# Two of the seven products of a paired feed-forward pass take both halves of their moving data in one 512-column matmul

## The chip, the core and the metric

The kernel runs on one core of a Trainium2 chip, as one program for two transformer stacks. The metric is the device time of one execution in microseconds (us). Before the change it is 3205.59 us, the median of three runs (3205.07 to 3207.72). The engines of the core work in parallel and meet through semaphores: TensorE (PE, with its weight loads as PEld), VectorE (DVE), ScalarE (ACT), GpSimd (POOL), and SyncE (SP), which issues most DMAs.

## The reference, cut to what matters

All tensors are float32, 512 tokens of width 1024. Among attention and mixer layers there are six gated feed-forward layers of hidden width 2816, and the change touches the input side of these:

```python
gate, up = jnp.split(h @ w_ffn_in[l], 2, axis=-1)          # two layers of the first stack
f = (jax.nn.silu(gate) * up) @ w_ffn_out[l]

def _swiglu(h, wg, wu, wd):                                # four of the second stack
    return (jax.nn.silu(h @ wg) * (h @ wu)) @ wd
```

## The kernel before

A float32 product is made of three products of a reduced format (fp32r). Each operand is split into a high part, which ScalarE casts, and a low part, which VectorE or GpSimd gets by subtracting the high part. A product then is w_hi x high + w_hi x low + w_lo x high, accumulated in a PSUM bank of 128 x 512 float32.

The input side of a feed-forward layer (a pass, below) has 22 gate tiles and 22 up tiles of 128 columns. The first five of each are done plainly, as ten units. The other 17 of each are "pairs" p = 0 to 16: a gate tile and the up tile of the same hidden columns are computed together as a 2 x 2 block product by a Strassen-like scheme with seven products instead of eight. The weight of a pair is split in A11, A12 (gate row) and A22 and A21 (up row), and four sums S1 to S4 are formed from them. The moving side has seven forms, B11, T1, T2, B21, B22, T3, T4, each of 4 k-tiles x 256 columns, made once a pass and kept with their high and low parts. The products in TensorE's order within `period(t, p)` are: A11 x B11, S1 x T1, A22 x T4 of the pair before (`fourth`), S2 x T2, A12 x B21, S4 x B22, S3 x T3. One product is twelve matmuls of 256 columns: `product` alternates high (L2771) and low (L2773) moving parts on the same w_hi block, four times, and then runs four with w_lo (L2777). Products on the chain go to bank 4 (odd p) or 6 (even p), `chain_bank`. The others share bank 5 or 7, `side_bank`: A12 x B21 in its left half, S1 x T1 and S4 x B22 in its right half.

While TensorE works on pair p, the other engines prepare pair q = p + 1 and finish p. Their order is the order of the code in each engine's `period`:

- ScalarE (L1161 on): a copy of the chain bank after product 1 (L1170, the first copy), S3's high part, A11's high part of q, a copy of S1 x T1 (`fifth_copy`, L1144), S1's high part, A22's, a copy of the chain (`sixth_copy`, L1153), S2's, A12's, then the silu of the gate (`silu_pair`, L1149), then S4's high part. High parts are L1127.
- VectorE (L1853 on): A11's low part, the sum S1, the hidden product of the pair before (L1835), A22's low part, the sum S2, the low parts of S1 of q and of S3 of p in one instruction of 1024 columns, A12's low part, the gate sum (L1895: side bank plus the two copies, which gives bank_free), the sum S4 (`fourth_sum`), the last half (L1850, which releases T4's product by st_u), the sum S3, the low parts of S2 and S4. Sums are L1806, low parts L1799.

The silu waits for bank_free of its pair. TensorE's w_lo matmuls of S3 in pair p wait for the low parts made in the same pair (`n_lo` 11 of a pair's seven counts, so four of the next seven); all the other weights are prepared a pair ahead. Each engine runs in order, so an instruction that waits holds all behind it. The first and last pairs are written out, and those between run as a hardware loop of two pairs (`pair_loop`). SyncE loads 512 KB for each row of a pair into a ring of four slots, released by st_sum and st_lo.

At the start of a pass VectorE builds the forms, ScalarE casts their high parts (`form_high`, L1124) and VectorE subtracts the low ones (`form_low`, L1795). A form's low part is written over its full value. High parts of B21 and B22 lie in the two halves of one four-tile region of mvh, those of T3 and T4 in the same region of mvl; these tiles are free once the ten plain units are done.

## Time and profile before

| | value |
|---|---|
| runs | 3205.07, 3205.59, 3207.72 us |
| the profiled execution | 3205.14 us, its span 3203.4 us |
| TensorE busy | 3157.5 us, 99% of the span, 19226 matmuls |
| TensorE's mean granted clock | 0.999 of full speed |
| VectorE, ScalarE, GpSimd busy | 2011.4, 1511.4, 1096.5 us |
| chain that ended last | TensorE 89%, VectorE 5%, ScalarE 2%, GpSimd 2%, issue 2% |
| matmuls of the paired part (L2771, L2773, L2777) | 8568 of 256 columns |

A matmul's row in the timeline has a modelled end: rows of consecutive matmuls overlap, so durations of matmuls are not their cost. The distance between starts is. VectorE's and ScalarE's rows also overlap by some hundredths of a microsecond, and there too the slot is the distance between starts.

### The profile page before, as it was taken

To read this page: it belongs to the slowest core of one execution; us is meant where nothing else is said; L and a number is where in the kernel's file an instruction comes from. 1 tells how busy PE (TensorE), PEld (TensorE's weight loads), DVE (VectorE), ACT (ScalarE), POOL (GpSimd) and SP (SyncE) were. 2 spreads that over 40 slices of the span, in tenths; PEclk is the share of its full clock that TensorE was granted. 3 is DMA by queue.
4 is the path that set the end of the run, shared out by engine and by line. 5 is a ranking of instruction groups with operands and counts; after the bars stand their busy time and mean duration, and the time that the engine had idled before them with its cause. 6 is when DMAs were issued, how large, how long until landed. Compare 5 with 4: busy or idle time off the path is not lost.

```text
span 3203.4 us, 53989 instructions
## 1 busy us (share of the span) xinstructions
PE 3157.5 (99%) x19226; PEld 2746.4 (86%) x19226; DVE 2011.4 (63%) x3103; ACT 1511.4 (47%) x2696; POOL 1096.5 (34%) x635
## 2 busy tenths in 40 slices
PE   9999999999999999999999999999999999999999
PEld 7678998786789987899888778998899887789987
DVE  4748874558488745888445247864688443348854
ACT  4655552557555524555333434552455333335542
POOL 5533014765340146500465341014400453350034
PEclk9999999999999999999999999999999999999999
DMA  4112332231123332232422122332232322122331
GB/s 158 53 47 87 109 114 97 86 103 53 47 86 105 112 104 80 80 105 92 154 92 86 53 73 80 105 118 98 79 103 90 129 94 71 61 86 93 103 118 66
DMA packets 82433, 294.27 MB, mean 92 GB/s; under 512 B 9035, under 2 KB 11467, under 8 KB 82028
## 3 DMA queue, kind: packets, MB, share of 16 engines
q1 hardware_dynamic: 80944, 286.06, 26.6%
q10 hardware_dynamic: 1340, 6.23, 0.5%
q8 instruction: 93, 1.52, 0.2%
q14 instruction: 56, 0.46, 0.1%
HBM read 290.15 MB, written 2.10 MB: 91 GB/s over the span
## 4 chain that ended last, share of the span: by engine, by line
PE 89%; DVE 5%; issue 2%; ACT 2%; POOL 2%; DMA 0%; SPq 0%; POOLq 0%; DVEq 0%; ACTq 0%
PE bank L2553 17%; PE bank L2555 17%; PE bank L2554 17%; PE bank L2777 10%; PE bank L2773 10%; PE bank L2771 10%; PE bank L3176 1%; PE bank L3156 1%; DVE w_lo L1799 1%; POOL w_lo L745 1%; ACT w_hi L1127 1%; PE bank L3263 1%; POOL diag L880 1%; PE bank L3018 1%; PE bank L3298 0%
## 5 line engine op out<-in xcount | busy, mean ns | idle before, releaser
L745 POOL TENSOR_TENSOR w_lo<-w_raw,w_hi 128x1024 fp32r<-128x1024 f32 (+1 forms) x334 | 790.3, 2375 | 1851.6 <-ACT w_hi L974 1807.6
L2553 PE MATMUL bank<-mvh,w_hi 128*128 128x512 f32 (+1 forms) x2774 | 1057.0, 381 | 10.3 <-DVE mvl L1708 2.9
L2555 PE MATMUL bank<-mvh,w_lo 128*128 128x512 f32 (+1 forms) x2774 | 1034.5, 373 | 0.0
L2554 PE MATMUL bank<-mvl,w_hi 128*128 128x512 f32 (+1 forms) x2774 | 1033.8, 373 | 0.0
L974 ACT ACTIVATE w_hi<-w_raw 128x1024 fp32r<-128x1024 f32 x333 | 351.1, 1058 | 799.2 <-PE bank L2555 759.3
L2553 PEld LDWEIGHTS bank<-mvh,w_hi 128*128 128x128 f32 x2774 | 522.3, 188 | 135.4 <-issue 35.2
L2555 PEld LDWEIGHTS bank<-mvh,w_lo 128*128 128x128 f32 x2774 | 522.2, 188 | 93.8
L2554 PEld LDWEIGHTS bank<-mvl,w_hi 128*128 128x128 f32 x2774 | 523.0, 189 | 84.9 <-issue 0.2
L1964 DVE TENSOR_TENSOR mvl<-big,mvh 128x512 fp32r<-128x512 f32 x108 | 255.8, 2368 | 327.4 <-ACT mvh L1261 327.4
L1127 ACT ACTIVATE w_hi<-w_lo_as 128x512 fp32r<-128x512 f32 x408 | 256.1, 630 | 202.1 <-DVE w_lo_as L1806 201.9
L2773 PE MATMUL bank<-y_as,w_hi 128*128 128x256 f32 x1224 | 306.9, 283 | 0.0
L2773 PE MATMUL bank<-big_as,w_hi 128*128 128x256 f32 x1224 | 306.8, 283 | 0.0
L1799 DVE TENSOR_TENSOR w_lo<-w_raw,w_hi 128x512 fp32r<-128x512 f32 x306 | 210.9, 689 | 95.1 <-ACT w_hi L1127 93.0
L1799 DVE TENSOR_TENSOR w_lo<-w_lo_as,w_hi 128x1024 fp32r<-128x1024 f32 (+1 forms) x216 | 250.6, 1162 | 11.2 <-DVE w_lo_as L1806 1.6
L2773 PEld LDWEIGHTS bank<-y_as,w_hi 128*128 128x128 f32 x1224 | 235.0, 192 | 0.2
L2773 PEld LDWEIGHTS bank<-big_as,w_hi 128*128 128x128 f32 x1224 | 234.9, 192 | 0.0
L2771 PE MATMUL bank<-mvl,w_hi 128*128 128x256 f32 x816 | 205.1, 284 | 1.7 <-DVE bank L1850 1.7
L2771 PE MATMUL bank<-mvh,w_hi 128*128 128x256 f32 x816 | 204.8, 283 | 0.0
L2771 PE MATMUL bank<-tab_as,w_hi 128*128 128x256 f32 x816 | 204.6, 283 | 0.0
L1127 ACT ACTIVATE w_hi<-w_raw 128x512 fp32r<-128x512 f32 x306 | 189.1, 618 | 3.5 <-issue 3.5
L880 POOL TENSOR_TENSOR diag<-diag,scr 128x512 f32<-128x512 f32 (+1 forms) x144 | 160.5, 1115 | 19.0 <-ACT scr L992 3.3
L2771 PEld LDWEIGHTS bank<-mvl,w_hi 128*128 128x128 f32 x816 | 156.5, 192 | 3.1 <-DVE bank L1850 2.9
(287 smaller groups left out, 4676.8 us busy)
## 6 DMA issues: line engine op xcount, KB each, us to landing
w_raw<-in_weights SPq DMA_DIRECT2D x537, 512.0 KB, 3.3
x<-in_x SPq DMA_DIRECT2D x8, 256.0 KB, 7.6
out_y<-y SPq DMA_DIRECT2D x8, 256.0 KB, 2.4
tab<-in_dist ACTq DMA_DIRECT2D x2, 640.0 KB
tab<-in_gmlp ACTq DMA_DIRECT2D x2, 640.0 KB
tab<-in_ret_dil ACTq DMA_DIRECT2D x1, 1280.0 KB
y<-in_p ACTq DMA_DIRECT2D x2, 512.0 KB, 3.5
y<-in_rotary ACTq DMA_DIRECT2D x1, 1024.0 KB
```

Of the source, the lines that this page charges most:

```text
L745: last = nc.gpsimd.tensor_tensor(w_lo[:, slot, at], w_raw[:, slot, at], w_hi[:, slot, at].bitcast(F32), ALU.subtract)
L880: nc.gpsimd.tensor_tensor(at, at, sq_at(name, i), ALU.add).then_inc(sq_used, 1)
L974: nc.scalar.activation(w_hi[:, slot, :], w_raw[:, slot, :], ACT.Copy).then_inc(w_hi_ready, 1)
L1127: nc.scalar.activation(st.hi(form), src, ACT.Copy).then_inc(st_hi, more)
L1799: nc.vector.tensor_tensor(st.lo(form, n), src, st.hi(form, n).bitcast(F32), ALU.subtract).then_inc(st_lo, more)
L1964: nc.vector.tensor_tensor(mvl[:, slot0 + s % 4, :], src, mvh[:, slot0 + s % 4, :].bitcast(F32), ALU.subtract).then_inc(mv_lo, 1)
L2553: nc.tensor.matmul(bank[:, at], hi, mvh[:, k, at], start=first, stop=False, skip_group_check=again)
L2554: nc.tensor.matmul(bank[:, at], hi, mvl[:, k, at], start=False, stop=False, skip_group_check=again)
L2555: return nc.tensor.matmul(bank[:, at], lo, mvh[:, k, at], start=False, stop=last, skip_group_check=again)
L2771: nc.tensor.matmul(bank, w, high[:, k, :], start=(begin and k == 0), stop=False, skip_group_check=True)
L2773: nc.tensor.matmul(bank, w, low[:, k, :], start=False, stop=False, skip_group_check=True)
L2777: last = nc.tensor.matmul(bank, w, high[:, k, :], start=False, stop=(k == 3), skip_group_check=True)
```

## The change

In pairs 1 to 15 (`wide`), the eight matmuls of a product with w_hi and the form B21 or B22 become four of 512 columns, whose moving operand holds the high part and the low part side by side (`both`). The bank then holds high-part columns at left and low-part columns at right. The two products take banks of their own: 0 and 1 in odd pairs, 2 and 3 in even pairs (`left_bank`, `side_bank`), with S1 x T1 in the left half of the second. VectorE adds the left halves of both banks to the copies (gate_begun), then the sum S4 is made, then it adds the right halves, which gives bank_free. To have high and low of B21 and of B22 adjacent, the low parts go beside the high parts, in mvh and mvl, and the high parts of T3 and T4 go where the full values and low parts of B21 and B22 were; ScalarE's casts of T3 and T4 therefore wait for form_lo. `down_first`, the start of the output side, waits for pair 15's bank_free, since it uses banks 0 to 3.

```diff
@@ -217,7 +217,8 @@
         gvar = small[:, 308:312]
         ret_vars = small[:, 232:248]
 
-        banks = [ctx.enter_context(nc.psum_tensor(f"bank{i}", [P, 512], F32)) for i in range(8)]
+        bank = ctx.enter_context(nc.psum_tensor("bank", [P, 8, 512], F32))
+        banks = [bank[:, i, :] for i in range(8)]
 
 
         x_loaded, p_loaded = [sem(f"x_loaded{i}") for i in range(KT)], sem("p_loaded")
@@ -287,6 +288,7 @@
         st_sum, st_hi, st_lo = sem("st_sum"), sem("st_hi"), sem("st_lo")
         st_prod, st_copy, st_u = sem("st_prod"), sem("st_copy"), sem("st_u")
         form_sum, form_hi, form_lo = sem("form_sum"), sem("form_hi"), sem("form_lo")
+        gate_begun = sem("gate_begun")
 
         def ge(eng, s, v):
 
@@ -589,7 +591,8 @@
                 m = 4 if name[0] == "a" else 0
                 wide = lambda t: t.rearrange("p a (b c) -> p (a b) c", c=S // 2)
                 late = [wide(t[:, m + j:m + j + 2, :]) for t in (mvh, mvl) for j in (0, 2)]
-
+                self.both = {f: t[:, m:m + 4, :].rearrange("p (j a) (b c) -> p j (a b) c", j=2, c=S // 2)
+                             for f, t in ((B21, mvh), (B22, mvl))}
 
                 def homes(y, big, scr):
                     ys = [wide(y[:, 2 * j:2 * j + 2, :]) for j in range(1, 4)]
@@ -602,7 +605,8 @@
                 pair = lambda t: t.rearrange("p (s a) (b c) -> p s (a b) c", s=2, c=S // 2)
                 self.normal = [pair(y[:, 2:6, :]), pair(big[:, FT:FT + 4, :])]
                 self.high = {B11: wide(scr_r[:, 8:10, :]), T1: tabs[0], T2: tabs[1]}
-                self.high.update(zip((B21, B22, T3, T4), late))
+                self.high.update({B21: late[0], B22: late[2], T3: self.low[B21], T4: self.low[B22]})
+                self.low.update({B21: late[1], B22: late[3]})
 
             def block(self, of, form, n=1):
                 at = (2 * (self.slot0 % RING) + form) % 8
@@ -626,7 +630,21 @@
                 return banks[4 if p % 2 else 6]
 
             def side_bank(self, p):
-                return banks[5 if p % 2 else 7]
+                return banks[7 if not self.wide(p) else 1 if p % 2 else 3]
+
+            def wide(self, p):
+
+                return 0 < p < PAIRS_ST - 1
+
+            def left_bank(self, p):
+                return banks[0 if p % 2 else 2]
+
+            def right(self, p):
+                return self.side_bank(p)[:, 0:S // 2] if self.wide(p) else self.side_bank(p)[:, S // 2:S]
+
+            def sides(self, p, part):
+                at = 0 if p % 2 else 2
+                return bank[:, at:at + 2, part * S // 2:(part + 1) * S // 2]
 
         def pair_loop(eng, first, last, body):
 
@@ -1121,6 +1139,8 @@
                 def form_high(form):
                     order = (B11, T1, T2, T3, B22, B21, T4)
                     act.wait_ge(form_sum, st.form0 + order.index(form) + 1)
+                    if form in (T3, T4):
+                        act.wait_ge(form_lo, st.form0 + (4 if form == T3 else 5))
                     nc.scalar.activation(st.high[form], st.full[form], ACT.Copy).then_inc(form_hi, 1)
 
                 def high(form, src, more=1):
@@ -1141,7 +1161,7 @@
                     product_done(t, p, 2)
                     if p >= 2:
                         act.wait_ge(st_u, t * 2 + st.u_0 + p - 1)
-                    nc.scalar.activation(fifth[:, p % 2, :], st.side_bank(p)[:, S // 2:S], ACT.Copy).then_inc(st_copy, 1)
+                    nc.scalar.activation(fifth[:, p % 2, :], st.right(p), ACT.Copy).then_inc(st_copy, 1)
 
                 def silu_pair(t, p):
                     act.wait_ge(bank_free, t * 2 + st.g0 + p + 1)
@@ -1892,10 +1912,18 @@
                         last_half(t, p)
                     product_done(t, p, 6)
                     dve.wait_ge(st_copy, t * 6 + st.copy0 + 3 * p + 3)
-                    nc.vector.tensor_tensor(g1[:, p % 2, :], st.side_bank(p)[:, :], parted[:, (p + 1) % 2, :],
-                                            ALU.add).then_inc(bank_free, 1)
-                    if more:
+                    if st.wide(p):
+                        halves = lambda a: a.rearrange("p (j c) -> p j c", j=2)
+                        g, b = halves(g1[:, p % 2, :]), halves(parted[:, (p + 1) % 2, :])
+                        nc.vector.tensor_tensor(g, st.sides(p, 0), b, ALU.add).then_inc(gate_begun, 1)
                         fourth_sum(t, q)
+                        dve.wait_ge(gate_begun, t * 2 + (PAIRS_ST - 2) * st.i + p)
+                        nc.vector.tensor_tensor(g, st.sides(p, 1), g, ALU.add).then_inc(bank_free, 1)
+                    else:
+                        nc.vector.tensor_tensor(g1[:, p % 2, :], st.side_bank(p)[:, :], parted[:, (p + 1) % 2, :],
+                                                ALU.add).then_inc(bank_free, 1)
+                        if more:
+                            fourth_sum(t, q)
                     if p:
                         last_half(t, p)
                     if more:
@@ -2766,8 +2794,15 @@
                         pe.wait_ge(form_lo, st.form0 + order.index(form) + 1)
                     pe.wait_ge(st_hi, t * 14 + st.hi0 + 7 * p + n_hi)
                     high, low = st.high[form], st.low[form]
+                    both = st.both[form] if form in st.both and st.wide(p) else None
+                    if both is not None:
+                        whole, bank = bank, bank[:, 0:S // 2]
                     for k in range(4):
                         w = st.hi(weight)[:, k * P:(k + 1) * P]
+                        if both is not None:
+                            nc.tensor.matmul(whole.rearrange("p (j c) -> p j c", j=2), w, both[:, :, k, :],
+                                             start=(begin and k == 0), stop=False, skip_group_check=True)
+                            continue
                         nc.tensor.matmul(bank, w, high[:, k, :], start=(begin and k == 0), stop=False,
                                          skip_group_check=True)
                         nc.tensor.matmul(bank, w, low[:, k, :], start=False, stop=False, skip_group_check=True)
@@ -2788,22 +2823,24 @@
                     pe.wait_ge(st_copy, t * 6 + st.copy0 + 3 * p + n)
 
                 def period(t, p):
-                    chained, left, right = (st.chain_bank(p)[:, 0:S // 2], st.side_bank(p)[:, 0:S // 2],
-                                            st.side_bank(p)[:, S // 2:S])
+                    chained, left, right = st.chain_bank(p)[:, 0:S // 2], st.side_bank(p)[:, 0:S // 2], st.right(p)
+                    fifth_at, third_at = right, right
+                    if st.wide(p):
+                        left, third_at = st.left_bank(p)[:, :], st.side_bank(p)[:, :]
                     if p == 1:
                         pe.wait_ge(bank_free, st.g0)
                     elif p:
                         pe.wait_ge(hidden_ready, t * 2 + st.f0 + p - 1)
                         pe.wait_ge(bank_free, t * 2 + st.g0 + p - 1)
                     product(t, p, chained, A11, 2, 1 if p < 2 else 2, B11, True)
-                    product(t, p, right, S1, 3 if p < 2 else 4, 2 if p == 1 else 4, T1, True, 1 if p else 2)
+                    product(t, p, fifth_at, S1, 3 if p < 2 else 4, 2 if p == 1 else 4, T1, True, 1 if p else 2)
                     if p:
                         fourth(t, p - 1)
                     copied(t, p, 1)
                     product(t, p, chained, S2, 5 if p else 6, 7, T2, False)
                     copied(t, p, 2)
-                    product(t, p, left, A12, 6 if p else 7, 5, B21, False)
-                    product(t, p, right, S4, 7 if p else 8, 7, B22, False)
+                    product(t, p, left, A12, 6 if p else 7, 5, B21, st.wide(p))
+                    product(t, p, third_at, S4, 7 if p else 8, 7, B22, False)
                     copied(t, p, 3)
                     product(t, p, chained, S3, 8 if p else 4, (4, 8)[p] if p < 2 else 11, T3, False)
 
@@ -2828,6 +2865,7 @@
 
                 pe.wait_ge(w_hi_ready, L.u0 + 1)
                 pe.wait_ge(mv_lo, L.m0 + 1)
+                pe.wait_ge(bank_free, st.g0 + PAIRS_ST - 1)
                 high(0)
                 high(1)
                 pe.wait_ge(w_lo_ready, L.u0 + 1)
```

The instructions move as follows. TensorE, pair 1, the product of A12 with B21 before (mvh high, big_as low, w_hi and w_lo weights):

```order
L2771 MATMUL bank<-mvh,w_hi 128x256 [waits st_hi,st_copy]
L2773 MATMUL bank<-big_as,w_hi 128x256
L2771 MATMUL bank<-mvh,w_hi 128x256
L2773 MATMUL bank<-big_as,w_hi 128x256
L2771 MATMUL bank<-mvh,w_hi 128x256
L2773 MATMUL bank<-big_as,w_hi 128x256
L2771 MATMUL bank<-mvh,w_hi 128x256
L2773 MATMUL bank<-big_as,w_hi 128x256
L2777 MATMUL bank<-mvh,w_lo 128x256 [waits st_lo]
L2777 MATMUL bank<-mvh,w_lo 128x256 x3
```

and now, with the product of S4 and B22 (mvl) behind it:

```order
L2803 MATMUL bank<-mvh,w_hi 128x512 [waits st_hi,st_copy]
L2803 MATMUL bank<-mvh,w_hi 128x512 x3
L2812 MATMUL bank<-mvh,w_lo 128x256 [waits st_lo]
L2812 MATMUL bank<-mvh,w_lo 128x256 x3
L2803 MATMUL bank<-mvl,w_hi 128x512 [waits st_hi]
L2803 MATMUL bank<-mvl,w_hi 128x512 x3
L2812 MATMUL bank<-mvl,w_lo 128x256 [waits st_lo]
L2812 MATMUL bank<-mvl,w_lo 128x256 x3
```

Eight rows of w_hi matmuls of 256 columns became four of 512; the four with w_lo are as they were.

VectorE, second pair of the loop body, around the gate sum (scr<-bank,scr), before. The row behind the gate sum is the sum S4, bank<-bank,scr is the last half, and the last row shown is the low parts of S2 and S4:

```order
L1799 TENSOR_TENSOR w_lo<-w_raw,w_hi 128x512 [waits st_hi]
L1894 REGISTER_ALU [waits st_prod]
L1895 TENSOR_TENSOR scr<-bank,scr 128x512 [waits st_copy]
L1806 TENSOR_TENSOR w_lo_as<-w_lo_as,w_raw 128x512 [waits st_sum]
L1850 TENSOR_TENSOR bank<-bank,scr 128x256 [waits st_prod]
L1806 TENSOR_TENSOR w_lo_as<-w_raw 128x512
L1803 REGISTER_ALU
L1799 TENSOR_TENSOR w_lo<-w_lo_as,w_hi 128x1024 [waits st_hi]
```

and now:

```order
L1819 TENSOR_TENSOR w_lo<-w_raw,w_hi 128x512 [waits st_hi]
L1914 REGISTER_ALU [waits st_prod]
L1918 TENSOR_TENSOR scr<-bank,scr 128x512 [waits st_copy]
L1826 TENSOR_TENSOR w_lo_as<-w_lo_as,w_raw 128x512 [waits st_sum]
L1921 TENSOR_TENSOR scr<-bank,scr 128x512 [waits gate_begun]
L1870 TENSOR_TENSOR bank<-bank,scr 128x256 [waits st_prod]
L1826 TENSOR_TENSOR w_lo_as<-w_raw 128x512
L1823 REGISTER_ALU
L1819 TENSOR_TENSOR w_lo<-w_lo_as,w_hi 128x1024 [waits st_hi]
```

A second operation of 512 columns stands between the sum S4 and the last half, with a wait of its own on gate_begun.

ScalarE at the start of a pass, before: the casts of B21 and B22, the first copy, T3's cast (from y), the fifth-product copy, T4's cast (from scr), A11's high part:

```order
L1124 ACTIVATE mvh<-big 128x1024 [waits form_sum,unit_done]
L1124 ACTIVATE mvh<-big 128x1024 [waits form_sum]
L1170 ACTIVATE scr<-bank 128x256 [waits hidden_ready,st_prod]
L1124 ACTIVATE mvl<-y 128x1024 [waits form_sum]
L1144 ACTIVATE scr<-bank 128x256 [waits st_prod]
L1124 ACTIVATE mvl<-scr 128x1024 [waits form_sum]
L1127 ACTIVATE w_hi<-w_raw 128x512 [waits st_gate_loaded1]
```

and now:

```order
L1144 ACTIVATE mvh<-big 128x1024 [waits form_sum,unit_done]
L1144 ACTIVATE mvl<-big 128x1024 [waits form_sum]
L1190 ACTIVATE scr<-bank 128x256 [waits hidden_ready,st_prod]
L1144 ACTIVATE big_as<-y 128x1024 [waits form_lo,form_sum]
L1164 ACTIVATE scr<-bank 128x256 [waits st_prod]
L1144 ACTIVATE big_as<-scr 128x1024 [waits form_lo,form_sum]
L1147 ACTIVATE w_hi<-w_raw 128x512 [waits st_gate_loaded1]
```

The order is the same; the casts of T3 and T4 have another destination and wait for form_lo as well, with the copies of pair 0 queued between and behind them.

## Rows read from the trace of the kernel before

**Rows 1.** The page: busy time, share of the span and instructions by engine.

```profile
PE 3157.5 (99%) x19226; PEld 2746.4 (86%) x19226; DVE 2011.4 (63%) x3103; ACT 1511.4 (47%) x2696; POOL 1096.5 (34%) x635
```

**Rows 2.** The timeline of TensorE (start us, us, engine, line, operation, wait before).

```profile
499.64 0.39 PE L2554 MATMUL bank<-mvl,w_hi 128*128 128x512 f32 x1
...
500.32 0.39 PE L2554 MATMUL bank<-mvl,w_hi 128*128 128x512 f32 x1
...
316.02 0.28 PE L2771 MATMUL bank<-scr_as,w_hi 128*128 128x256 f32 x1
...
457.14 0.28 PE L2771 MATMUL bank<-scr_as,w_hi 128*128 128x256 f32 x1
```

**Rows 3.** The timeline of steady pairs, ScalarE, VectorE and TensorE.

```profile
337.90 0.38 ACT L1170 ACTIVATE scr<-bank 128x256 f32<-128x256 f32 x1 [0.92 <-PE bank L2777]
...
343.27 1.23 DVE L1799 TENSOR_TENSOR w_lo<-w_lo_as,w_hi 128x1024 fp32r<-128x1024 f32 x1
...
345.78 0.64 PE L2777 MATMUL bank<-mvl,w_lo 128*128 128x256 f32 x4
```

**Rows 4.** The timeline, VectorE and ScalarE, first pass, pair 1 to 2.

```profile
316.50 0.68 DVE L1895 TENSOR_TENSOR scr<-bank,scr 128x512 f32<-128x512 f32 x1
...
317.10 0.68 DVE L1806 TENSOR_TENSOR w_lo_as<-w_lo_as,w_raw 128x512 f32<-128x512 f32 x1
...
317.22 0.63 ACT L1149 ACTIVATE scr<-scr 128x512 f32<-128x512 f32 x1 [1.36 <-DVE scr L1895]
...
317.70 0.43 DVE L1850 TENSOR_TENSOR bank<-bank,scr 128x256 f32<-128x256 f32 x1
...
317.82 0.63 ACT L1127 ACTIVATE w_hi<-w_lo_as 128x512 fp32r<-128x512 f32 x1
...
318.36 0.37 ACT L1170 ACTIVATE scr<-bank 128x256 f32<-128x256 f32 x1
...
319.29 0.62 ACT L1127 ACTIVATE w_hi<-w_raw 128x512 fp32r<-128x512 f32 x1
...
319.94 0.69 DVE L1799 TENSOR_TENSOR w_lo<-w_raw,w_hi 128x512 fp32r<-128x512 f32 x1
...
320.55 0.68 DVE L1806 TENSOR_TENSOR w_lo_as<-w_raw 128x512 f32<-128x512 f32 x1
...
322.46 0.69 DVE L1799 TENSOR_TENSOR w_lo<-w_raw,w_hi 128x512 fp32r<-128x512 f32 x1 [0.62 <-ACT w_hi L1127]
...
323.06 0.68 DVE L1806 TENSOR_TENSOR w_lo_as<-w_lo_as,w_raw 128x512 f32<-128x512 f32 x1
...
323.85 1.23 DVE L1799 TENSOR_TENSOR w_lo<-w_lo_as,w_hi 128x1024 fp32r<-128x1024 f32 x1
...
325.60 0.68 DVE L1895 TENSOR_TENSOR scr<-bank,scr 128x512 f32<-128x512 f32 x1
```

**Rows 5.** The timeline, all engines, start of the first pass.

```profile
298.34 1.05 ACT L1124 ACTIVATE mvl<-y 128x1024 fp32r<-128x1024 f32 x1
...
298.76 2.36 DVE L1795 TENSOR_TENSOR big_as<-big,mvh 128x1024 fp32r<-128x1024 f32 x2
...
299.29 0.37 ACT L1144 ACTIVATE scr<-bank 128x256 f32<-128x256 f32 x1
...
299.55 1.06 ACT L1124 ACTIVATE mvl<-scr 128x1024 fp32r<-128x1024 f32 x1
...
300.27 0.32 PE L2771 MATMUL bank<-mvh,w_hi 128*128 128x256 f32 x1
...
302.16 1.22 DVE L1795 TENSOR_TENSOR scr_as<-scr,mvl 128x1024 fp32r<-128x1024 f32 x1
...
307.94 0.38 PE L2771 MATMUL bank<-mvl,w_hi 128*128 128x256 f32 x1 [0.27 <-DVE bank L1850]
...
311.12 0.74 PE L2777 MATMUL bank<-tab_as,w_lo 128*128 128x256 f32 x4 [0.53 <-DVE w_lo L1799]
...
311.70 0.28 PE L2771 MATMUL bank<-mvh,w_hi 128*128 128x256 f32 x1
```

## The prediction

> **What bounds the kernel now.** I read the page's totals first: TensorE is busy for 99% of the span, VectorE for 63%, ScalarE for 47% [rows 1]. So a shorter stream of matmuls pays in full, and any new wait of TensorE costs in full. Next I read TensorE's cadence in the timeline, by starts, since the ends are modelled. A 512-column matmul takes a slot of (500.32 - 499.64)/3 = 0.2267 us. In the paired part a pair is 84 matmuls of 256 columns, and TensorE begins the products of pair 2 at 316.02 and those of pair 16 at 457.14, which is 14 pairs of 10.08 us, 0.1200 us a matmul [rows 2]. Two 256-column slots are 0.2400, one 512-column slot is 0.2267: a wide matmul is worth 0.0133 us.
>
> Then I asked who runs beside TensorE. Each pair, VectorE and ScalarE prepare the next pair's weights: sums (L1806), high parts (L1127), low parts (L1799). In the steady state this is in time but not by much. The low parts of S1 and S3 start at 343.27 and last 1.23, to 344.50, and the matmuls that need S3's (L2777) start at 345.78: 1.3 us of slack, while ScalarE's first copy of a pair sits idle 0.92 until TensorE releases it [rows 3]. So TensorE paces the loop, and VectorE follows with about one microsecond to spare.
>
> How fast VectorE and ScalarE would go if TensorE didn't pace them is shown once, at the start, where they are behind. From the gate sum of pair 1 (316.50) to that of pair 2 (325.60) they run without a wait on TensorE: 9.10 us [rows 4]. That is the number on which this prediction rests. The path goes: gate sum 316.50, silu 317.22 (it waits for the sum), S4's high part 317.82, first copy 318.36, A11's high part 319.29, its low part 319.94, the next S1 sum 320.55, A22's low part 322.46 (through two casts of ScalarE), the S2 sum 323.06, the S1/S3 low parts 323.85, A12's low part, and the next gate sum. The silu stands on this path because ScalarE executes it ahead of S4's cast and of all that follows: nothing needs its result soon, but everything is queued behind it.
>
> **The change, part by part.**
>
> Matmuls: of 17 pairs of a pass, pairs 1 to 15 are wide, so 90 in six passes. Each replaces 16 matmuls of 256 columns by 8 of 512 and saves 8 x 0.0133 = 0.107 us. TensorE's own work of a wide pair becomes 10.08 - 0.107 = 9.97 us, and 90 of them are 9.6 us less, if nothing else binds.
>
> Here the Trainium skill speaks against the change (TensorE: Matmul & The Clock Gate, "Back-to-back issue gap"): its isolated gap when warm is N/2.4 + 2.5 ns, so merging two matmuls would save only 2.5 ns, not the 13.3 that the rows give. By the page the sum of this item would be an estimated 90 x 8 x 0.0025 = 1.8 us. The trace does not agree with it, and I take the trace.
>
> VectorE: the gate sum (512 columns, two inputs) becomes two such sums, with the fourth sum between them. The silu now waits for the second. On the path above this adds two slots, that of the fourth sum and that of the second add, both ahead of the silu. The fourth sum's slot is measured: 317.10 to 317.70, 0.60. The second add is not in the trace. It is of the same kind and size as the first, which takes the slot 316.50 to 317.10, 0.60. The bounds: an add of half the size lasts 0.43 instead of 0.68, 0.25 less, which gives 0.35; an operation that waits for VectorE's own preceding one takes 323.06 to 323.85, 0.79 [rows 4]. The new wait (gate_begun) is for an operation that started 1.20 earlier and lasts 0.68, so it should be met. I take 0.60.
>
> The Trainium skill has a rule for this slot (VectorE: DVE Perf Modes, "The DRAIN you can't avoid"): the next operation does not start until the pipe is empty. Then each slot would be the full 0.68 to 0.69, and the two added ones together 0.17 more. The rows show starts 0.60 apart under durations of 0.68, so I use the starts.
>
> So the loop of VectorE and ScalarE that was 9.10 becomes 9.10 + 0.60 + 0.60 = 10.30 us a pair. TensorE needs 9.97. The follower has become the slower one, and also slower than the 10.08 of before.
>
> Start of a pass: the high parts of T3 and T4 move to where the full B21 and B22 stand, so ScalarE must wait for their low parts. B21's low part starts at 298.76; two take 2.36, one alone about 1.22, to 299.98. T3's cast, 298.34 before, starts at 300.02. The cast and what follows it take 299.29 - 298.34 = 0.95, so the fifth-product copy queued behind it starts at 300.97 instead of 299.29, lasts 0.38 and ends at 301.35. TensorE waits for it before the A12 product, which started at 300.27: it now starts near 301.4, and with the slower first slot loses 1.2 us [rows 5]. But TensorE stalled later anyway: at 307.94 and 311.12, for VectorE (0.27 and 0.53 idle). Expected starts follow from 0.1200 a matmul; counted so, with the first slots after a wait, the two stalls cost about 1.3. VectorE itself moves by only 0.17: T4's cast follows the copy by 299.55 - 299.29 = 0.26, at 301.23, lasts 1.06 to 302.29, and T4's low part starts at 302.33 instead of 302.16. The matmuls at 311.12 start at about 311.29. So the 1.2 falls into the old stalls, and what passes on is VectorE's 0.17. Pair 2's products start at 311.29 + 0.58 + 1.387 x 2 + 1.44 = 316.08 instead of 316.02 (1.387 is a wide product, 4 x 0.2267 + 4 x 0.1200; 0.58 is from the start of the four low matmuls to the next product after such a wait, 311.12 to 311.70) [rows 5]. The wait itself is priced between 0 (if the whole 1.2 is absorbed) and 1.2 us a pass, 7 in all.
>
> Pairs 2 to 15: the gate sum of pair 1 starts at 316.50 + 0.17 = 316.67, and each next one 10.30 later. What TensorE waits for is S3's low part in the same pair. It starts 323.85 - 316.50 = 7.35 after the gate sum before, now 8.55, lasts 1.23, plus 0.05 until the matmul: 9.83. The next pair's products start 0.58 later: 10.41 after that gate sum. Pair 16 starts at 316.67 + 13 x 10.30 + 10.41 = 460.98 instead of 457.14: 3.84 us later. The six passes start alike, so 6 x 3.84 = 23.0 us.
>
> End of a pass: pair 16 is not wide and has no next pair to prepare. VectorE and ScalarE start it late, but the sums and casts of a next pair are missing there, so S3's low part is ready before its matmuls, and the products of w_ffn_out follow as before. If that cover fails it costs a wait of the kind above, 0.2 to 1 us a pass. The new wait of down_first for bank_free is for pair 15's second add, done some 8 us before. No stall goes there, and I price both at 0. Weight loads are released by the same low parts and land in the same 10 us, so they stay ahead; 0. The casts' destinations change and their sizes don't; 0.
>
> Sum: 3205.1 (the profiled execution; its span is 3203.4, and the median of the runs is 3205.6) + 23.0 = 3228 us. Slower by 0.7%.
>
> **The rivals.**
>
> TensorE remains the bound, faster (other side). If the second add and the silu don't lengthen the path, TensorE's 9.97 paces: the slot of 10.30 would have to be wrong by 0.33. For it: VectorE alone gets 0.6 us more work a pair, and the loop had 10.08 - 9.10 = 0.98 to spare. Against: the 9.10 is a measured free run and not a sum of estimates. A loop at or under 9.97 gives 6 x (0.06 - 14 x 0.107) = -8.6: 3196.5 us. The skill's 2.5 ns would make it an estimated 3204. Chance 0.10.
>
> The loop binds at the lower bound of the add, 0.35. Then it is 10.05: pair 16 starts at 316.67 + 130.65 + 10.16 = 457.48, 0.34 late, 2 us in all: 3207. This counts as no change. Chance 0.07.
>
> The loop is longer than I think. With 0.79 for the add it is 10.49 and pair 16 comes 14 x 0.19 = 2.7 later still: 16 us more, 3244. The turn of the hardware loop every second pair belongs here: before, it was hidden under waits like the 0.92 at 337.90 [rows 3], so it may cost 0 to 0.9 in each of about 6 turns; the entry into the loop lies in the free run, between S4's cast at 317.82 and the copy 0.54 later, and cost nothing visible. With 0.3 each it is 11 us more, 3239. Chance of clearly more than my forecast's own spread (above 3243): 0.13.
>
> That the wide matmuls are no faster than two narrow ones would not matter to my forecast: TensorE has 0.33 us a pair to spare under a loop of 10.30. It would only remove the gain of the first rival.
>
> **How the numbers follow.** The forecast has a chance of 0.70 with a range of its own from 3214 to 3243 (a slot error of 0.1 us a pair is 8.4 us). The first rival has 0.10, the second 0.07, the third 0.13. Within 0.2% means within 6.4 us, about what a measurement of this kernel can tell from no change. Faster: 0.10. Same: the second rival, 0.07. Slower: 0.83. The range leaves out the faster case and a part of the longest: 3208 to 3246.
>
> **What would show it right or wrong.** Right: in steady pairs the gate sums stand 10.3 us apart; the silu starts about 1.9 us after the first gate sum instead of 0.72; ScalarE's first copy no longer waits for TensorE; TensorE waits once a pair, some 0.2 us, on the low weight matmuls of S3 for VectorE's L1799 equivalent, about 84 times; its two start stalls give way to one near 301.4. Wrong: gate sums 9.97 apart with ScalarE's first copy still waiting for TensorE means that the path has a shortcut that I overlooked; gate sums over 10.5 apart mean a dearer add or loop turn.

## The result

The changed kernel takes 3210.14 us, median of 22 runs (3208.92 to 3211.36), against 3205.75 (3204.48 to 3207.72, 22 runs) before: ratio 1.0014, 95% interval 1.0007 to 1.002. It is 4.4 us slower. The sign was forecast, the size was not: 23 us were forecast. The measured time lies inside the range, which began at 3208, but near its lower end.

The page after, the same line as in [rows 1]: engine, busy us, share and instructions. 720 matmuls are gone, and TensorE's busy time, modelled, hardly changed.

```profile
PE 3157.3 (98%) x18506; PEld 2710.2 (84%) x18506; DVE 2048.6 (64%) x3193; ACT 1477.9 (46%) x2696; POOL 1097.4 (34%) x635
```

VectorE in the timeline after, pairs 1 to 3 of the first pass; some rows between are left out. They are the gate sum (L1918), the sum S4 (L1826), the second add (L1921), the sum S3 (L1826 again), A11's low part, the low parts of S1 and S3, the next two gate sums.

```profile
317.32 0.69 DVE L1918 TENSOR_TENSOR scr<-bank,scr 128x512 f32<-128x512 f32 x1
317.92 0.68 DVE L1826 TENSOR_TENSOR w_lo_as<-w_lo_as,w_raw 128x512 f32<-128x512 f32 x1
318.52 0.68 DVE L1921 TENSOR_TENSOR scr<-bank,scr 128x512 f32<-128x512 f32 x1
...
319.45 0.68 DVE L1826 TENSOR_TENSOR w_lo_as<-w_raw 128x512 f32<-128x512 f32 x1
...
321.73 0.69 DVE L1819 TENSOR_TENSOR w_lo<-w_raw,w_hi 128x512 fp32r<-128x512 f32 x1
...
325.64 1.23 DVE L1819 TENSOR_TENSOR w_lo<-w_lo_as,w_hi 128x1024 fp32r<-128x1024 f32 x1
...
327.38 0.68 DVE L1918 TENSOR_TENSOR scr<-bank,scr 128x512 f32<-128x512 f32 x1
...
337.45 0.69 DVE L1918 TENSOR_TENSOR scr<-bank,scr 128x512 f32<-128x512 f32 x1
```

ScalarE in the same stretch: the silu (L1169), S4's cast, the first copy (L1190), S3's cast, A11's cast.

```profile
319.23 0.63 ACT L1169 ACTIVATE scr<-scr 128x512 f32<-128x512 f32 x1 [2.56 <-DVE scr L1921]
319.77 0.62 ACT L1147 ACTIVATE w_hi<-w_lo_as 128x512 fp32r<-128x512 f32 x1
320.29 0.36 ACT L1190 ACTIVATE scr<-bank 128x256 f32<-128x256 f32 x1
320.56 0.62 ACT L1147 ACTIVATE w_hi<-w_lo_as 128x512 fp32r<-128x512 f32 x1
321.08 0.62 ACT L1147 ACTIVATE w_hi<-w_raw 128x512 fp32r<-128x512 f32 x1
```

The gate sums stand 10.06 and 10.07 us apart, where [rows 4] had 9.10; from pair 1 to pair 15 they take 140.93 to 140.96 us in each of the six passes, 10.066 a pair. The silu starts 1.91 after the gate sum instead of 0.72, and the first copy no longer waits for TensorE as in [rows 3]. TensorE waits for S3's low part in pair 2, at the start of its four low matmuls:

```profile
326.92 0.74 PE L2812 MATMUL bank<-big_as,w_lo 128*128 128x256 f32 x4 [0.43 <-DVE w_lo L1819]
```

In pair 3 no wait is listed, and yet time is lost. The low parts there, the four low matmuls and the next product, and the same two rows of TensorE in pair 4:

```profile
335.70 1.23 DVE L1819 TENSOR_TENSOR w_lo<-w_lo_as,w_hi 128x1024 fp32r<-128x1024 f32 x1
...
337.02 0.69 PE L2812 MATMUL bank<-big_as,w_lo 128*128 128x256 f32 x4
337.67 0.38 PE L2806 MATMUL bank<-scr_as,w_hi 128*128 128x256 f32 x1
...
347.29 0.64 PE L2812 MATMUL bank<-big_as,w_lo 128*128 128x256 f32 x4
347.77 0.28 PE L2806 MATMUL bank<-scr_as,w_hi 128*128 128x256 f32 x1
```

In pair 3 the low parts are done at 336.93, 0.09 before TensorE's low matmuls, and the next product follows those by 0.65. In pair 4 they are done 0.30 before, and it follows by 0.48. From pair 4 on, pairs of 10.01 us and of 10.07 to 10.16 alternate, which makes the mean of 10.054 in the table below. So TensorE pays for its slower follower in small portions that the list of waits doesn't show.

At the start of the pass (its instructions stand 0.6 us later in this trace than in [rows 5]: pair 0's start, as read below, is at 297.51 instead of 296.92): B21's low part, T3's cast waiting for it, the fifth-product copy behind that, TensorE waiting for the copy, and the low matmuls of S2 in pair 1, which waited 0.53 before and now show no wait.

```profile
299.36 1.22 DVE L1815 TENSOR_TENSOR mvh<-big,mvh 128x1024 fp32r<-128x1024 f32 x1
...
300.67 1.06 ACT L1144 ACTIVATE big_as<-y 128x1024 fp32r<-128x1024 f32 x1 [1.63 <-DVE mvh L1815]
301.63 0.37 ACT L1164 ACTIVATE scr<-bank 128x256 f32<-128x256 f32 x1
...
302.05 0.39 PE L2806 MATMUL bank<-mvh,w_hi 128*128 128x256 f32 x1 [1.02 <-ACT scr L1164]
...
311.94 0.74 PE L2812 MATMUL bank<-tab_as,w_lo 128*128 128x256 f32 x4
```

TensorE's waits on these lines in the whole run (us in total, times, longest):

```profile
PE bank L2806 <- ACT scr L1164: 6.1, 6, 1.0
...
PE bank L2812 <- DVE w_lo L1819: 2.6, 6, 0.4
```

The pair starts say where the time went. The start of pair p is read as the first of the four matmuls of A11 x B11 with low weights (the operand is scr_as, w_lo), less the same start of pair 0. First pass, us, for all the kernels below:

| kernel | pair 1 | pair 2 | pair 3 | pair 4 | pair 16 | mean of the last 12 pairs |
|---|---|---|---|---|---|---|
| before | 8.67 | 20.06 | 30.14 | 40.22 | 161.18 | 10.080 |
| after | 9.91 | 20.22 | 30.95 | 41.21 | 161.86 | 10.054 |
| silu later | 9.90 | 20.19 | 30.57 | 40.57 | 160.65 | 10.007 |
| fifth-product copy first | 8.70 | 20.10 | 30.86 | 41.13 | 161.81 | 10.057 |
| second add alone, on before | 8.67 | 20.06 | 30.72 | 41.00 | 161.96 | 10.080 |
| without the second add | 9.92 | 20.22 | 30.22 | 40.23 | 160.31 | 10.007 |
| before, silu later | 8.66 | 20.06 | 30.14 | 40.22 | 161.18 | 10.080 |
| silu later, copy first | 8.68 | 20.14 | 30.49 | 40.50 | 160.58 | 10.007 |
| second add first | 9.90 | 20.18 | 30.70 | 40.72 | 160.79 | 10.006 |
| homes alone, on before | 9.91 | 20.29 | 30.37 | 40.45 | 161.41 | 10.080 |
| wide, adjacent columns | 9.92 | 20.19 | 30.58 | 40.58 | 160.66 | 10.007 |
| both orders, pair 1 narrow | 8.69 | 20.20 | 30.21 | 40.21 | 160.29 | 10.007 |

After the change a pass is 161.86 - 161.18 = 0.68 us longer; six make 4.1 of the 4.4 us. Of it 0.16 is there at pair 2, 0.83 more comes in pairs 2 and 3, and the twelve after give back 12 x 0.026 = 0.31.

### The profile page after: what moved, and what is told of

It reads as the page before. It is cut to its first block, busy times and chain, and to the rows that moved or that the text cites. A ratio compares the mean times of both kernels' runs of the same rounds, so it can differ in the third digit from the quotient of the medians.

```text
span 3208.3 us, 52711 instructions
## 1 busy us (share of the span) xinstructions
PE 3157.3 (98%) x18506; PEld 2710.2 (84%) x18506; DVE 2048.6 (64%) x3193; ACT 1477.9 (46%) x2696; POOL 1097.4 (34%) x635
## 4 chain that ended last, share of the span: by engine, by line
PE 87%; DVE 5%; issue 3%; ACT 3%; POOL 2%; DMA 0%; DVEq 0%; ACTq 0%; SPq 0%; POOLq 0%
PE bank L2581 17%; PE bank L2583 17%; PE bank L2582 17%; PE bank L2812 9%; PE bank L2806 7%; PE bank L2808 7%; PE bank L2803 5%; DVE w_lo L1819 1%; ACT w_hi L1147 1%; PE bank L3214 1%; PE bank L3194 1%; POOL w_lo L763 1%; DVE w_lo_as L1826 1%; PE bank L3301 1%; POOL diag L898 1%
## 5 line engine op out<-in xcount | busy, mean ns | idle before, releaser
L2581 PE MATMUL bank<-mvh,w_hi 128*128 128x512 f32 (+1 forms) x2774 | 1057.0, 381 | 10.6 <-DVE mvl L1728 2.9
L2581 PEld LDWEIGHTS bank<-mvh,w_hi 128*128 128x128 f32 x2774 | 522.4, 188 | 136.0 <-issue 35.2
L2582 PEld LDWEIGHTS bank<-mvl,w_hi 128*128 128x128 f32 x2774 | 523.1, 189 | 84.9 <-issue 0.2
L2806 PE MATMUL bank<-big_as,w_hi 128*128 128x256 f32 x816 | 204.8, 283 | 0.0
L1169 ACT ACTIVATE scr<-scr 128x512 f32<-128x512 f32 x102 | 64.5, 632 | 243.6 <-DVE scr L1921 231.9
L2806 PEld LDWEIGHTS bank<-big_as,w_hi 128*128 128x128 f32 x816 | 156.5, 192 | 0.3
L2806 PEld LDWEIGHTS bank<-tab_as,w_hi 128*128 128x128 f32 x816 | 156.6, 192 | 0.0
L1826 DVE TENSOR_TENSOR w_lo_as<-w_lo_as,w_raw 128x512 f32<-128x512 f32 x204 | 139.4, 683 | 6.9 <-PE bank L2583 6.1
```

The costliest lines, as they stand in the source:

```text
L2581: nc.tensor.matmul(bank[:, at], hi, mvh[:, k, at], start=first, stop=False, skip_group_check=again)
L2582: nc.tensor.matmul(bank[:, at], hi, mvl[:, k, at], start=False, stop=False, skip_group_check=again)
L2806: nc.tensor.matmul(bank, w, high[:, k, :], start=(begin and k == 0), stop=False, skip_group_check=True)
```

## The experiments

Each was timed against the kernel before on the same chip (3205.60 to 3205.80 there); the changed kernel is compared by its 3210.14, which was measured apart. The 95% interval of a ratio is about 0.0009 to either side, some 3 us, so differences under that rest on the traces and the table, not on the times. The diffs show only the lines that matter, with "..." between them.

**Silu later** (e1): 3202.50 us, ratio 0.999 (0.9981 to 0.9999).

```diff
                     if p:
                         fifth_copy(t, p)
+                    if p > 1:
+                        silu_pair(t, p - 1)
...
                     if p:
-                        silu_pair(t, p)
+                        if q == PAIRS_ST:
+                            silu_pair(t, p)
                         if q < PAIRS_ST:
                             sum_high(t, q, S4)
```

> The changed kernel, with the silu of pair p moved from ahead of S4's cast to the next pair, behind the fifth-product copy, so that nothing which the weights need is queued behind it. Theory A (the silu holds ScalarE's casts until VectorE's second add is done, and this path of about 10.07 us a pair, not TensorE, paces pairs 2 to 15): gate sums go to 9.97 us apart after the first two pairs, the silu path's lag of about 0.7 us a pass shrinks to about 0.35, and pair 16 starts about 1.0 us earlier a pass than in the kernel before: about 3199.5 us. Theory B (a 512-column matmul saves nothing over two of 256, so TensorE itself needs 10.07 a pair): gate sums stay 10.07 apart, 3208 to 3210. Theory C (the loss is the new wait of 1.0 us at A12 x B21 of pair 0, six times): 3210, unchanged.

The loss turns into a gain of 3.1 us, 7.6 less than the changed kernel. Pairs run at 10.007. That rejects B (a wide matmul saves nothing) and C (the start wait is the loss: it is still there, 6.1 us in six times). The value is 3 us above the forecast of A, since 10.007 is not the 9.97 that was put in. The wide products in this trace, four matmuls of 512 and four of 256:

```profile
342.35 1.09 PE L2806 MATMUL bank<-mvh,w_hi 128*128 128x512 f32 x4
343.28 0.63 PE L2815 MATMUL bank<-mvh,w_lo 128*128 128x256 f32 x4
```

Four wide ones take 0.93 us from start to start, 0.2325 each, not 0.2267. Two products of a pair so save 8 x 0.0075 = 0.060; a pair saves 0.073, as the four low matmuls behind take 0.47 instead of 0.48. Expected were 0.107.

**Fifth-product copy first** (e2): 3209.67, ratio 1.0012 (1.0003 to 1.0021).

```diff
+                        fifth_copy(t, p)
                         form_high(T3)
-                        fifth_copy(t, p)
                         form_high(T4)
```

> The changed kernel, with ScalarE's fifth-product copy of pair 0 put ahead of the casts of T3 and T4. Theory A (the wait of 1.0 us at A12 x B21 of pair 0 stands in place of two older waits for VectorE in pair 1, so it costs almost nothing): that wait goes, the older ones at A22 x T4 and at the low weights of S2 in pair 1 come back with about 0.3 and 0.5 us idle, 3209 to 3210 us. Theory C (this wait is the loss): about 3204.

Theory A holds. Pair 1 starts at 8.70 again, pair 2 at 20.10, and the two waits for VectorE are back (TensorE's waits; L1870 is the last half):

```profile
PE bank L2812 <- DVE w_lo L1819: 5.8, 12, 0.5
...
PE bank L2806 <- DVE bank L1870: 2.4, 6, 0.4
```

The wait of 6.1 us that the profile after puts first among TensorE's waits was worth about 0.5 by the times, too little for them to tell from nothing, and 0.05 a pass by the table.

**Second add alone, on the kernel before** (e3): 3210.00, ratio 1.0013 (1.0004 to 1.0022).

```diff
                     nc.vector.tensor_tensor(g1[:, p % 2, :], st.side_bank(p)[:, :], parted[:, (p + 1) % 2, :],
-                                            ALU.add).then_inc(bank_free, 1)
+                                            ALU.add).then_inc(gate_begun if wide else bank_free, 1)
                     if more:
                         fourth_sum(t, q)
+                    if wide:
+                        g = g1[:, p % 2, :]
+                        dve.wait_ge(gate_begun, t * 2 + (PAIRS_ST - 2) * st.i + p)
+                        nc.vector.tensor_tensor(g, g, g, ALU.max).then_inc(bank_free, 1)
```

> The kernel before (narrow matmuls, old homes), with a second VectorE operation of 512 columns, max(g, g), behind the sum S4 in pairs 1 to 15, and bank_free given by it. Theory A: VectorE and ScalarE follow TensorE by 10.06 instead of 9.10 us a pair; TensorE stays at 10.08, but the lag of pair 1 is no longer made up before S3's low part is needed in pair 2: TensorE waits there once, about 0.5 us a pass, pair 16 starts about 0.6 later, about 3209 us. Theories B and C: VectorE has room for it, nothing waits, 3205.7.

All of the loss, with none of the matmuls changed and no new wait at the start of a pass. VectorE, gate sum, the extra operation, the next gate sums:

```profile
317.50 0.68 DVE L1897 TENSOR_TENSOR scr<-bank,scr 128x512 f32<-128x512 f32 x1
...
318.70 0.69 DVE L1904 TENSOR_TENSOR scr<-scr 128x512 f32<-128x512 f32 x1
...
327.57 0.68 DVE L1897 TENSOR_TENSOR scr<-bank,scr 128x512 f32<-128x512 f32 x1
...
337.64 0.68 DVE L1897 TENSOR_TENSOR scr<-bank,scr 128x512 f32<-128x512 f32 x1
```

From pair 1 to pair 2 the gate sums now stand 10.07 apart where [rows 4] had 9.10, against TensorE's 10.08. The starts of pairs 3 and 4 come late (by 0.58, and 0.20 more), and nothing is made up after.

**Without the second add** (e4): 3200.27, ratio 0.9983 (0.9974 to 0.9992).

```diff
-                        nc.vector.tensor_tensor(g, st.sides(p, 0), b, ALU.add).then_inc(gate_begun, 1)
+                        nc.vector.tensor_tensor(g, st.sides(p, 0), b, ALU.add).then_inc(bank_free, 1)
                         fourth_sum(t, q)
-                        dve.wait_ge(gate_begun, t * 2 + (PAIRS_ST - 2) * st.i + p)
-                        nc.vector.tensor_tensor(g, st.sides(p, 1), g, ALU.add).then_inc(bank_free, 1)
```

> The changed kernel without the second add: the gate sum takes the left halves alone and gives bank_free (the low-part columns of two products are left out of the gate). Theory A: VectorE and ScalarE are back at 9.1 us a pair, TensorE paces at 9.97: pair 16 starts about 1.3 us earlier a pass than in the kernel before, about 3197.6 us. Theory B: pairs stay at 10.07 or 10.08, 3206 to 3207. Theory C: gain of the matmuls less 6 us of start waits, about 3202.

Theory A holds, again with 10.007 for the pair. The kernel leaves the low-part columns of two products out of the gate. Its gain is what the wide matmuls bring without the second add: 5.3 us, of the 9.6 that two narrow slots against one wide slot of the plain units promised. The start wait is in it and costs 0.16 a pass at pair 2.

**Before, silu later** (e5): 3205.61, ratio 1.0 (0.999 to 1.0009). The edit is that of e1.

> The kernel before, with the silu moved behind the next pair's fifth-product copy. Two readings of the free run of 9.10 us from pair 1 to pair 2: (A) the silu lies beside that path, and VectorE's four operations up to the sum S3 set it (S4's and S3's casts each waited a little for their sums), so without the silu it stays 9.0 to 9.1; (B) the silu lies on it, as the prediction took it, and 9.10 falls to about 8.5. TensorE paces at 10.08 either way: 3205.7 us, no change, in both.

The time was to be the same in both readings; the trace decides. The rows are the gate sum of pair 1, S4's cast, sum S3, S3's cast, the silu in its new place, and the gate sum of pair 2:

```profile
316.51 0.68 DVE L1898 TENSOR_TENSOR scr<-bank,scr 128x512 f32<-128x512 f32 x1
...
317.83 0.63 ACT L1127 ACTIVATE w_hi<-w_lo_as 128x512 fp32r<-128x512 f32 x1 [1.96 <-DVE w_lo_as L1809]
...
318.05 0.68 DVE L1809 TENSOR_TENSOR w_lo_as<-w_raw 128x512 f32<-128x512 f32 x1
...
318.76 0.63 ACT L1127 ACTIVATE w_hi<-w_lo_as 128x512 fp32r<-128x512 f32 x1
...
320.08 0.62 ACT L1149 ACTIVATE scr<-scr 128x512 f32<-128x512 f32 x1
...
325.60 0.69 DVE L1898 TENSOR_TENSOR scr<-bank,scr 128x512 f32<-128x512 f32 x1
```

The gate sums stand 9.09 apart, where [rows 4] had 9.10, although no silu stands ahead of the casts. S4's cast starts 1.32 after the gate sum, as before, and S3's 2.25 after it, as before. In its new place the silu (0.62 long) falls into a gap of ScalarE, whose next cast at 321.27 has another 0.57 of idle time ahead of it, so it did not merely move along the path. So the silu was not on the free path: S3's cast starts when the sum S3 ends (318.05 + 0.68), and that sum set the path as far as S3's cast in the kernel before too.

**Both orders** (e6: the edits of e1 and e2): 3202.01, ratio 0.9989 (0.998 to 0.9998).

> The changed kernel with both orders moved: the silu behind the next pair's fifth-product copy, and pair 0's fifth-product copy ahead of the casts of T3 and T4. Theory A (start wait at A12 x B21 only stands in for two older waits): as with the silu alone, 3202.5 us or up to 0.4 less. Theory C (that wait counts): 3197.

That is A's forecast: C would have had 3197. The start wait is worth 0.5 us by the times, within their noise, and 0.07 a pass by the table.

**Second add first** (e7): 3203.10, ratio 0.9992 (0.9983 to 1.0001). VectorE's work is that of the changed kernel.

```diff
-                        fourth_sum(t, q)
                         dve.wait_ge(gate_begun, t * 2 + (PAIRS_ST - 2) * st.i + p)
                         nc.vector.tensor_tensor(g, st.sides(p, 1), g, ALU.add).then_inc(bank_free, 1)
+                        fourth_sum(t, q)
```

> The changed kernel with VectorE's second add directly behind the first (it then waits for it) and the sum S4 behind both. Theory A: the silu starts about 1.5 us after the gate sum instead of 1.9, S4's cast about 2.1 instead of 2.45; VectorE and ScalarE need about 9.9 us a pair, less than TensorE's 10.01 (measured with the silu out of the way), so pairs 4 to 15 run at 10.01 and the late pairs 2 and 3 stay: about 3204 us, between 3202.5 and 3210. If the silu's delay were not the cause but VectorE's amount of work, it would stay at 3210.

The timeline of VectorE and ScalarE shows the gate sum, second add, silu, and the next gate sum.

```profile
317.64 0.68 DVE L1918 TENSOR_TENSOR scr<-bank,scr 128x512 f32<-128x512 f32 x1
...
318.35 0.69 DVE L1920 TENSOR_TENSOR scr<-bank,scr 128x512 f32<-128x512 f32 x1
...
319.08 0.63 ACT L1169 ACTIVATE scr<-scr 128x512 f32<-128x512 f32 x1 [2.08 <-DVE scr L1920]
...
327.45 0.68 DVE L1918 TENSOR_TENSOR scr<-bank,scr 128x512 f32<-128x512 f32 x1
```

The silu starts 1.44 after the gate sum, and the free loop is 9.81 us, under TensorE's 10.007. Swapping two operations recovers 7.0 us against the changed kernel: the order of VectorE's work made the loss, not its amount.

**Homes alone, on the kernel before** (e8): 3206.74, ratio 1.0004 (0.9995 to 1.0013).

```diff
-                self.high.update(zip((B21, B22, T3, T4), late))
+                self.high.update({B21: late[0], B22: late[2], T3: self.low[B21], T4: self.low[B22]})
+                self.low.update({B21: late[1], B22: late[3]})
...
                     act.wait_ge(form_sum, st.form0 + order.index(form) + 1)
+                    if form in (T3, T4):
+                        act.wait_ge(form_lo, st.form0 + (4 if form == T3 else 5))
```

> The kernel before with only the forms' homes moved, and the casts of T3 and T4 waiting for form_lo. Theory A: one new wait of 1.0 us a pass at A12 x B21 of pair 0, the older waits of pair 1 shrink by nearly as much, pair 2 starts 0.15 us later a pass: 3206.5 us. Theory C: 6 us more than before, 3211.5.

It is 1.1 us slower, with six waits of 1.0 us at A12 x B21 in the profile (L2774, the first matmul):

```profile
PE bank L2774 <- ACT scr L1147: 6.1, 6, 1.0
```

By the table it is 0.23 a pass, 1.4 us in all. The interval of the ratio takes in no change, so the cost rests on the table.

**Wide, adjacent columns** (e9, on the kernel of e1): 3202.92, ratio 0.9991 (0.9982 to 1.0).

```diff
-                            nc.tensor.matmul(whole.rearrange("p (j c) -> p j c", j=2), w, both[:, :, k, :],
+                            source = mvh if form == B21 else mvl
+                            m = 4 if name[0] == "a" else 0
+                            nc.tensor.matmul(whole, w, source[:, m + k, :],
```

> As the changed kernel with the silu moved, but the wide matmuls read 512 adjacent columns of one tile instead of two runs of 256 that lie 1024 columns apart (so the two products are of other columns than the forms'). It asks why a wide matmul took 0.2325 us there and 0.2267 in the plain units. Theory D (the jump inside the moving operand costs it): the slot falls to 0.2267, pairs to 9.96 us, the whole to about 3202.5 - 90 x 0.045 = 3198.5. Theory E (it is the neighbourhood, wide beside narrow): 0.2325 and 10.01 stay, 3202.5.

The two products are of other columns here, but of the same number. The 10.007 stays, so the jump inside the moving operand is not what makes the wide slot longer. E, the neighbourhood, is what is left. It was not tried by itself, but the trace of the kernel before has a place that speaks for it, where matmuls of 512 columns follow ones of 256 at the end of a pass:

```profile
471.51 0.40 PE L2822 MATMUL bank<-mvh,w_hi 128*128 128x512 f32 x1
...
472.90 0.39 PE L2822 MATMUL bank<-mvh,w_hi 128*128 128x512 f32 x1
...
474.26 0.39 PE L2553 MATMUL bank<-mvh,w_hi 128*128 128x512 f32 x1
```

The first six take 1.39 us, 0.232 each, and the next six 1.36, 0.227. Why stays open.

**Both orders, pair 1 narrow** (e10): 3200.11, ratio 0.9983 (0.9974 to 0.9992), the fastest of those that leave nothing out. The lines shown come on top of the edits of e6.

```diff
-                return 0 < p < PAIRS_ST - 1
+                return 1 < p < PAIRS_ST - 1
...
-                return banks[7 if not self.wide(p) else 1 if p % 2 else 3]
+                return banks[(5 if p % 2 else 7) if not self.wide(p) else 1 if p % 2 else 3]
...
-                        dve.wait_ge(gate_begun, t * 2 + (PAIRS_ST - 2) * st.i + p)
+                        dve.wait_ge(gate_begun, t * 2 + (PAIRS_ST - 3) * st.i + p - 1)
```

> The changed kernel with both orders moved (silu, fifth-product copy), and pair 1 narrow again with one gate sum, so 14 wide pairs a pass. Theory A: the second add in pair 1, where VectorE and ScalarE are late, is what made TensorE wait 0.38 us a pass for S3's low part in pair 2. Without it that wait goes and 0.07 of TensorE's gain is given up: 3202.3 - 6 x 0.3 = about 3200.5 us. Otherwise it is 3202.5 or more.

Pair 2 takes 10.01 instead of 10.35, and the time is 1.9 us under that of e6, as A had it. The gate sums of pairs 2 and 3, free of TensorE:

```profile
325.81 0.69 DVE L1921 TENSOR_TENSOR scr<-bank,scr 128x512 f32<-128x512 f32 x1
...
335.50 0.69 DVE L1921 TENSOR_TENSOR scr<-bank,scr 128x512 f32<-128x512 f32 x1
```

They stand 9.69 apart. With the silu gone from ahead of the casts, the second add lengthens the free loop of 9.10 by 0.59, one slot, and VectorE and ScalarE have 0.3 to spare under TensorE's 10.007.

## Why the prediction was wrong in its size

**What bounds the kernel: right.** The follower became the slower one, 10.066 against TensorE's 10.007. The experiments without the add and with the silu later show it from two sides.

**The loop of 10.30: the step that failed.** The prediction said "On the path above this adds two slots, that of the fourth sum and that of the second add, both ahead of the silu", and added 1.20 to 9.10. The slots were right: 317.32, 317.92, 318.52 after, 0.60 each. But the silu did not stand on the free path of 9.10. Two branches ran from the gate sum to S3's cast: silu, S4's cast and first copy on ScalarE, and S4's sum, last half and S3's sum on VectorE, and VectorE's was the later one. The rows that show it in the trace of before are the sum S3 and S3's cast:

```profile
318.04 0.68 DVE L1806 TENSOR_TENSOR w_lo_as<-w_raw 128x512 f32<-128x512 f32 x1
...
318.75 0.63 ACT L1127 ACTIVATE w_hi<-w_lo_as 128x512 fp32r<-128x512 f32 x1
```

The cast starts 0.03 after the sum is done (318.72) and 0.39 after the first copy at 318.36, where the changed kernel has 0.27 between the two. It stands 2.25 after the gate sum. S4's cast at 317.82 likewise starts just when the sum S4 is done ([rows 4], 317.10 + 0.68), and in e5 it starts no earlier without a silu. The change made ScalarE's branch the later one: S3's cast stands 320.56 - 317.32 = 3.24 after the gate sum. So the path to it grew by 0.99, not 1.20: the gaps of ScalarE, which the prediction had counted as path, took up the rest. Behind the cast another 0.03 went in the same way, and 9.10 + 0.96 = 10.06 was measured.

A loop wrong by 0.24 is a small error. But it stood between two paces, TensorE's 10.08 before and its own need now, so over 14 pairs and six passes it became 6 x 14 x 0.24 = 20 us, against a miss of 23.0 - 4.4 = 18.6 us. The prediction's own sensitivity, 8.4 us for 0.1, said as much, but its range took the error for one of the second add alone.

**The wide matmul: mis-sized.** 0.107 a pair was expected, 0.073 measured, because the slot of 0.2267 was read in a stream of wide matmuls only. The forecast did not depend on it, as it said. The 2.5 ns a matmul of the Trainium skill (TensorE: Matmul & The Clock Gate, "Back-to-back issue gap") would be an estimated 0.020 a pair; the trace gives 0.073 / 8 = 9 ns and disagrees with it.

**Start of a pass: right.** Expected was a wait near 301.4 that costs 1.2 and is swallowed by the two old ones, with 0.06 left at pair 2. Measured: the wait at 302.05 in a trace that is 0.6 later, 1.24 at pair 1, and 0.16 at pair 2. The homes alone cost 1.1 us in all, within the noise of the times.

**Pairs 2 and 3: right in kind.** Pair 3's products were expected 1.0 late; they came 0.81 late. From there the prediction let the lag grow by 0.22 a pair; it grew by 0.18 once, to pair 4, and then shrank by 0.026 a pair. The sign that TensorE would wait once a pair, about 84 times, did not come either: six waits are listed, one a pass, and behind them stand the small losses in every second pair.

**End of a pass: right.** No wait appeared there: behind the pass the first matmul of L2581 starts at 475.59, 16.22 after pair 16's start, where the same one (L2553 in the kernel before, at 474.26) came 16.16 after it.

**The rule on the pipe** (Trainium skill, VectorE: DVE Perf Modes, "The DRAIN you can't avoid") would have given the slots 0.68; they were 0.60, and it would have missed by more. The same section says that an operation which is not held starts earlier; the prediction left that out.

**The rivals.** The second, a loop of 10.05, came with the right number for the wrong reason: it took 0.35 for the add's slot, and the slot was 0.60. It gave 3207, and called it no change. A loop of 10.066 instead of 10.05 is 1.2 us more over 13 pairs and six passes. The loop turn of the hardware loop cost nothing that shows: the gate sums stand 10.06 and 10.07 apart throughout.

## What to carry to other kernels

A measured free run tells how long a loop takes, and not which of its branches is the longer one. When a change adds to one branch, look first which branch each joint waited for: an instruction that starts within hundredths of its operand's end was held by that operand, and not by the queue ahead of it. An operation whose result nobody needs soon should not stand ahead of those that are needed, in an engine's in-order queue: moving one silu was worth 7.6 us, more than the wide matmuls bring. And the longest wait in the profile (here six times 1.0 us) may only stand in for others; take it away and see which come back.

## What the runs showed of the hardware

- A matmul of 512 columns among matmuls of 256 took 0.2325 us, and 0.2267 in a stream of its kind (before: 499.64 to 500.32); reading two runs of 256 columns 1024 apart, or 512 adjacent ones, made no difference (pairs of 10.007 in both).
- A wait of VectorE on its own operation that was two instructions back cost nothing (slots of 0.60 in the changed kernel). On the operation just before, in e7, it cost 0.11: the slot 317.64 to 318.35 is 0.71.
- A VectorE operation that reads halves of two PSUM banks took 0.683 us in the changed kernel and 0.689 in e1, as one that reads a whole bank did (0.689 in the kernel before).
- TensorE lost time to an operand of VectorE that was ready 0.09 us before it was needed (0.65 from the four low matmuls to the next product, instead of 0.48), though the profile lists no wait there. With 0.30 in hand nothing was lost, and where the follower was faster (e1, e4, e7) every pair from pair 4 on took 10.00 to 10.02.
